# Attention outputs with the values stationary, two heads on column halves, and denominators that are spread and turned in place of the outputs

## The chip, the core and the metric

The kernel runs on one core of one Trainium2 chip. The time is the device time of one execution in microseconds, and the median of three runs before the change is 2227.28 us (2225.45 to 2228.44). Five engines run their own instruction queues and meet at semaphores: TensorE (PE; PEld is its weight load), VectorE (DVE), ScalarE (ACT), GpSimd (POOL) and SyncE (SP), which issues the loads.

## The reference, cut to what matters

A stack of four layers works on 256 tokens of width 1024, all in fp32. The first layer has a convolution and an attention to 256 memory rows (two pairs of heads) and a dense feed-forward part. The second has an attention in a window of 128 keys (12 query heads, six pairs, each head with a sink in its softmax), again two memory pairs, and a feed-forward part of eight experts. Two hybrid layers follow, each with three mixers: one of three dilated windows, one over blocks, and one to the memory, with sigmoid gates. The computation that the change touches is the same everywhere:

```python
HEAD_DIM, SEQ, BLOCK = 64, 256, 128

def memory_attention(q, q_g, mem_k, mem_v):
    q = rms_norm(q.reshape(b, s, MEM_HEADS, HEAD_DIM), q_g)
    sc = jnp.einsum('bshd,bmhd->bhsm', q, mem_k).astype(jnp.float32) * (HEAD_DIM ** -0.5)
    p = jax.nn.softmax(sc, axis=-1).astype(mem_v.dtype)
    o = jnp.einsum('bhsm,bmhd->bshd', p, mem_v)
...
# window attention: masked, biased scores, a sink beside the keys
    sink = jnp.broadcast_to(sinks..., sc.shape[:-1] + (1,))
    p = jax.nn.softmax(jnp.concatenate([sc, sink], axis=-1), axis=-1)[..., :-1]
    o = jnp.einsum('bnhgqc,bnchd->bnqhgd', p.astype(vv.dtype), vv).reshape(b, s, SWA_Q_WIDTH)
    return jnp.concatenate([o, m], axis=-1) @ w_out
...
# dilated mixer: three windows under one softmax; block mixer: causal here, since 256 tokens are one block
    w = jax.nn.softmax(jnp.stack(lses, axis=0), axis=0)
    o = jnp.einsum('gbsh,gbshd->bshd', w, jnp.stack(outs, axis=0).astype(jnp.float32))
```

## The kernel before, in words

Each engine has its program written out by hand in one block, and the order of the calls in it is the order of its queue. Tokens lie on partitions, in T = 2 tiles of P = 128; S = 256. Weights come from memory in panels of 512 KB. ScalarE rounds each to `whi` (`split_to`, L678), VectorE makes the rest `wlo` (L1195), and TensorE multiplies three products of the halves (L2083, L2136, in the hybrid layers' gates `gate`, L2646). A panel's split waits for the load, and TensorE waits for the split.

Attention goes in pairs of heads, 22 in all: two in the first layer (with other work between, `between`), eight in the window attention (six causal, two dense to the memory), six in each hybrid layer (causal, causal, the dilated pair with three causal parts, causal, dense, dense). A pair passes these steps. TensorE computes `scores` (L2222): K is 64, and the two heads of a pair lie on partitions 0 to 63 and 64 to 127, so on the two row halves of the array. VectorE masks them and takes the minimum of the negated scores (L1323). ScalarE takes the exponentials with their sums, `den`, a column for each head and token tile (`exps`, L774). TensorE turns the probabilities (`transposes`, L2241), and ScalarE and VectorE copy them to `PT` in SBUF (`copies`, L786 and L1341), so that keys lie on partitions. TensorE multiplies them with the values (`values`, L2255): a 128x128 block of probabilities is the stationary operand, 64 columns of values stream, and queries come out on partitions, six such matmuls for a causal part and eight for a dense pair. VectorE adds the sink's term to `den` (L1352, the window's heads only), takes the reciprocal of 128x4 (L1353) and multiplies the output out of PSUM with it into `att` (L1356, `scaled`). TensorE turns `att` so that head columns lie on partitions (`out_turn`, L2267, two transposes). ScalarE rounds the result to `chi` (L795) and VectorE makes `clo` (L1365), both `pair_out`. The output projections read `chi` and `clo`.

The two output banks are used in turn: `values` of a pair waits for `ofree`, which `pair_out` on VectorE counts up two pairs before. In the hybrid layers 24 gate panels are laid between the steps by hand; in the window attention nothing is laid between, and the calls are a loop over the pairs in which scores run two pairs ahead and values one behind the transposes.

Of the kernel before, what the change touches and what calls it, by code (L numbers as in the profile page):

```python
# [22 lines left out]
P = 128  # L23
T = 2
S = T * P
# [100 lines left out]
def build(nc, d):  # L126
    ctx = ExitStack()
    with ctx:
# [90 lines left out]
        tab = sb("tab", [1, 1 + MAXJOB], I32)  # L219
        assert cursor[0] <= 229344, cursor[0]  # L220
# [19 lines left out]
        class Signals:  # L240

            def __init__(self, q):
# [20 lines left out]
                self.ex = sem(q + "ex")  # L263
                self.scaled = sem(q + "scaled")
                self.oturn = sem(q + "oturn")
# [393 lines left out]
        def _(e):  # L659
# [98 lines left out]
            def attention(w, pairs, slots, out=output_bank, between=None, parts=False):  # L758
# [33 lines left out]
                def pair_out(i):  # L792

                    e.wait_ge(w.s.oturn, w.at("o", 1))
                    act(chi[:, pairs[i][3], :], out(w, w.n["o"])[:, S:2 * S], ACT.Copy).then_inc(w.s.ohi, 1)  # L795
                    w.n["o"] += 1
# [383 lines left out]
        def _(e):  # L1180
# [122 lines left out]
            def attention(w, pairs, slots, out=output_bank, scored=None, between=None, parts=False, bank=None):  # L1303
# [42 lines left out]

                def scaled(i):

                    _, _, den, sunk = pair_stats(stat, i, len(pairs[i][0]))
                    e.wait_ge(w.s.ex, w.at("a", i + 1))  # L1350
                    if pairs[i][3]:
                        w.link(v.tensor_tensor(den, den, sunk, ALU.add))  # L1352
                    w.link(v.reciprocal(den, den))  # L1353
                    e.wait_ge(w.s.pv, w.at("v", v0 - w.n["v"] + plan[i][2] // 2 + len(pairs[i][0]) + 2))
                    rows = [P, T, 2, HD]
                    v.tensor_tensor(att[:, w.n["u"] % 2, :].rearrange("p (t x k) -> p t x k", t=T, x=2),  # L1356
                                    out(w, w.n["u"])[:, 0:S].rearrange("p (t x k) -> p t x k", t=T, x=2),
                                    den.rearrange("p (x t) -> p t x", t=T).unsqueeze(3).to_broadcast(rows), ALU.mult
                                    ).then_inc(w.s.scaled, 1)
                    w.n["u"] += 1  # L1360

                def pair_out(i):
                    tile = pairs[i][4]
                    e.wait_ge(w.s.ohi, w.at("o", 1))
                    v.tensor_tensor(clo[:, tile, :], out(w, w.n["o"])[:, S:2 * S], chi[:, tile, :].bitcast(F32), ALU.subtract  # L1365
# [3 lines left out]
                if parts:  # L1369
                    return scores, copies, scaled, pair_out  # L1370
# [4 lines left out]
                for s in range(len(steps) + 2):  # L1375
# [7 lines left out]
                    if 1 <= s <= len(steps) and steps[s - 1][2]:  # L1383
                        scaled(steps[s - 1][0])
                    if s >= 2 and steps[s - 2][2]:
# [241 lines left out]
            scores, copies, scaled, pair_out = attention(  # L1627
# [9 lines left out]
            for i in range(10):  # L1637
# [10 lines left out]
                if 1 <= i < 9:  # L1648
                    scaled(i - 1)
                if i == 1:  # L1650
# [183 lines left out]
            for l in range(2):  # L1834
# [51 lines left out]
                scores, copies, scaled, pair_out = attention(  # L1886
# [1025 lines left out]
```

## Time and profile before

| | |
|---|---|
| median of three runs | 2227.28 us (2225.45 to 2228.44) |
| profiled execution: its own time, span | 2225.27 us, 2223.3 us |
| mean granted clock of TensorE | 0.997 |
| busy share of TensorE, its weight load, VectorE, ScalarE | 98%, 84%, 77%, 63% |
| memory read | 548.67 MB, 247 GB/s over the span |

The page's table of busy times and its chain are averages over stages with different limits. For each of the four places of attention the chain of waits shows what was waited for last, and the windows and forms show how full each engine was and how long one instruction took. A matmul's listed duration reaches from its start to its modelled end, so several overlap; its price is read from how far apart they start, or from a piece of the chain divided by its count. One fp32 matmul call counts as two in the trace.

### The profile page before, as it was taken

The page shows a single profiled execution, that of the slowest core. Times are in us where ns is not written, and L with a number is a line of the kernel's source. Part 1 is how long each engine was busy: PE and PEld are TensorE (multiplying, and loading weights), DVE is VectorE, ACT ScalarE, POOL GpSimd, SP SyncE. Part 2 cuts the span into 40 slices and gives each one's busy share as a digit, 9 for nine tenths or more (in the row PEclk, how much of TensorE's full clock was granted, in tenths as well). Part 3 has the DMA queues.
Part 4 walks back from the last instruction along what each step waited for, and adds up shares of the span by engine and source line. Part 5 has one row for each costly group of instructions (what it writes and reads, how often), then busy time and mean ns, then how long its engine had stood idle before and what let it go on. Part 6 is the DMA issues. An engine that isn't in the chain of part 4 may idle for free.

```text
span 2223.3 us, 36118 instructions
## 1 busy us (share of the span) xinstructions
PE 2185.2 (98%) x11690; PEld 1869.2 (84%) x11690; DVE 1716.8 (77%) x2249; ACT 1404.6 (63%) x1864; POOL 137.6 (6%) x142
## 2 busy tenths in 40 slices
PE   8999999999999999999999999999999999999998
PEld 7889987878888888888888888788889888888987
DVE  7956657699999999999999999866576556657654
ACT  4264446568787888878787878745645444564543
POOL 8400005020000000000000000000010000001000
PEclk9999999999999999999999999999999999999999
DMA  6236554279999999999999999854355655445564
GB/s 216 93 111 190 182 190 162 76 251 372 345 371 377 356 355 356 379 355 348 360 371 364 369 352 363 328 173 147 132 164 189 193 186 189 142 136 167 181 198 143
DMA packets 151054, 552.00 MB, mean 248 GB/s; under 512 B 16736, under 2 KB 16864, under 8 KB 150752
## 3 DMA queue, kind: packets, MB, share of 16 engines
q1 hardware_dynamic: 150448, 548.77, 69.6%
q8 instruction: 96, 1.57, 0.3%
q10 hardware_dynamic: 432, 1.02, 0.1%
q14 instruction: 78, 0.64, 0.1%
HBM read 548.67 MB, written 1.05 MB: 247 GB/s over the span
## 4 chain that ended last, share of the span: by engine, by line
PE 87%; issue 7%; DVE 3%; ACT 2%; POOL 0%; DMA 0%; DVEq 0%; ACTq 0%; POOLq 0%
PE L L2083 57%; PE L L2136 10%; PE L L2646 6%; PE L L2742 3%; PE TB L2151 2%; PE L L2100 2%; PE SC L2315 2%; PE L L2255 1%; DVE wlo L1195 1%; PE SC L2222 1%; PE TB L2241 1%; PE SC L2528 1%; PE SC L2536 1%; PE L L2365 1%; POOL stat L550 0%
## 5 line engine op out<-in xcount | busy, mean ns | idle before, releaser
L1195 DVE TENSOR_TENSOR wlo<-deep,whi 128x1024 fp32r<-128x1024 f32 x682 | 810.2, 1223 | 43.8 <-ACT whi L678 13.5
L678 ACT ACTIVATE whi<-deep 128x1024 fp32r<-128x1024 f32 x682 | 713.1, 1060 | 133.6 <-PE L L2083 130.0
L1195 DVE TENSOR_TENSOR wlo<-raw,whi 128x1024 fp32r<-128x1024 f32 x353 | 428.3, 1227 | 254.3 <-ACT whi L678 249.6
L678 ACT ACTIVATE whi<-raw 128x1024 fp32r<-128x1024 f32 x353 | 368.0, 1058 | 314.7 <-PE L L2083 154.6
L2083 PE MATMUL L<-whi,xhi 128*128 128x512 f32 (+1 forms) x1136 | 447.7, 394 | 3.1 <-DVE wlo L1195 2.7
L2083 PE MATMUL L<-whi,xlo 128*128 128x512 f32 (+1 forms) x1136 | 441.5, 389 | 0.0
L2083 PE MATMUL L<-wlo,xhi 128*128 128x512 f32 (+1 forms) x1136 | 441.2, 388 | 0.0
L2083 PEld LDWEIGHTS L<-whi,xhi 128*128 128x128 f32 x1136 | 213.7, 188 | 49.2 <-DVE wlo L1195 6.5
L2083 PEld LDWEIGHTS L<-whi,xlo 128*128 128x128 f32 x1136 | 213.6, 188 | 45.0
L2083 PEld LDWEIGHTS L<-wlo,xhi 128*128 128x128 f32 x1136 | 213.9, 188 | 42.0
L2083 PE MATMUL L<-whi,mhi 128*128 128x512 f32 x448 | 175.3, 391 | 0.0
L2083 PE MATMUL L<-wlo,mhi 128*128 128x512 f32 x448 | 174.6, 390 | 0.0
L2083 PE MATMUL L<-whi,mlo 128*128 128x512 f32 x448 | 174.3, 389 | 0.0
L2136 PE MATMUL L<-x2hi,whi 128*128 128x256 f32 x512 | 145.0, 283 | 0.0
L2136 PE MATMUL L<-x2hi,wlo 128*128 128x256 f32 x512 | 144.9, 283 | 0.0
L2136 PE MATMUL L<-x2lo,whi 128*128 128x256 f32 x512 | 144.9, 283 | 0.0
L2136 PE MATMUL L<-xhi,whi 128*128 128x256 f32 x448 | 128.0, 286 | 1.5 <-DVE xlo L1242 0.8
L2136 PE MATMUL L<-xhi,wlo 128*128 128x256 f32 x448 | 127.3, 284 | 0.0
L2136 PE MATMUL L<-xlo,whi 128*128 128x256 f32 x448 | 127.2, 284 | 0.0
L550 POOL TENSOR_TENSOR stat<-stat,halfneg 128x2 f32<-128x2 f32 (+3 forms) x18 | 22.4, 1246 | 1692.5 <-DVE stat L1216 1470.2
L2083 PE MATMUL L<-whi,fhi 128*128 128x512 f32 x280 | 109.7, 392 | 1.4 <-DVE wlo L1195 1.4
L2083 PE MATMUL L<-wlo,fhi 128*128 128x512 f32 x280 | 109.0, 389 | 0.0
(380 smaller groups left out, 3463.1 us busy)
## 6 DMA issues: line engine op xcount, KB each, us to landing
deep<-wm SPq DMA_DIRECT2D x679, 512.0 KB, 5.5
raw<-wm SPq DMA_DIRECT2D x245, 512.0 KB, 4.0
raw<-w SPq DMA_DIRECT2D x112, 512.0 KB, 4.3
mbuf<-mem SPq DMA_DIRECT2D x2, 1024.0 KB, 8.5
const<-const SPq DMA_DIRECT2D x1, 1312.0 KB, 8.7
out<-hn SPq DMA_DIRECT2D x2, 512.0 KB, 2.6
h<-x ACTq DMA_DIRECT2D x1, 512.0 KB, 4.9
h<-x SPq DMA_DIRECT2D x1, 512.0 KB, 4.8
```

The lines of the kernel that those rows point to most:

```text
L550: e.tensor_tensor(src, src, halfneg[:, 0:1].to_broadcast([P, n]), ALU.pow).then_inc(done, 1)
L678: act(hi, slots[:, slot, :], ACT.Copy).then_inc(w.s.hi, 1)
L1195: v.tensor_tensor(lo, slots[:, slot, :], hi.bitcast(F32), ALU.subtract).then_inc(w.s.lo, 1)
L2083: i = mm(L[2 * (g % 2) + t][:, 0:width], x[:, k, row], y[:, cols], start=(k == k0 and q == 0), stop=(k == k0 + n - 1 and q == 2))
L2100: i = mm(L[2 * (g % 2) + t][:, :], x[:, k, t * P:(t + 1) * P], y[:, kk * 512:(kk + 1) * 512], start=(k == 0 and q == 0), stop=(k == 2 * n ...
L2136: i = mm(out, x[:, cols], y[:, k, :], start=(k == 0 and q == 0 and f % 2 == 0), stop=(k == KD - 1 and q == 2 and f % 2 == 1), skip_group_c ...
L2151: i = tr(TB[w.n["t"] % 2][:, c:c + P], src, ident)
L2222: ins = mm(bank(w, x)[:, t * S:t * S + c], qkT[half, qp, t * P:(t + 1) * P], key[half, 0:c], start=True, stop=True)
L2241: ins = tr(TB[x][:, kt * S + t * P:kt * S + (t + 1) * P], tile[:, t, kt * P:(kt + 1) * P], ident)
L2315: ins = mm(SC[c % 2][:, f * S:(f + 1) * S], diag[2 * c + f][:, i, :], u[:, 2 * c + f, tap:tap + S], start=(i == 0), stop=(i == TAPS_PE - 1))
L2646: i = mm(L[2 * (bank % 2) + t][:, :], x[:, k, t * P:(t + 1) * P], y[:, kk * 512:(kk + 1) * 512], start=(k == 0 and q == 0), stop=(k == KD ...
L2742: i = mm(banks[t][:, :], x[:, k, t * P:(t + 1) * P], y[:, cols], start=(start and q == 0), stop=(stop and q == 2))
```

## The change

The operands of the values matmul change places: the values (128 keys x 64) are stationary, and the probabilities stream, 256 or 128 columns. The output is turned as it comes: head columns on partitions, the pair's first head on partitions 0 to 63 and its second on 64 to 127, so on the two column halves of the array. A causal part has four matmuls (of 256, 256, 128 and 128 columns) and a dense pair four of 256. Since queries are columns now, the denominator of a query has to stand in a column. VectorE spreads `den` over the 64 columns of each head into a new tile `dens`, 128x2x2x64 (`denominators`, with the sink's term added on the way), and TensorE turns that into the right half of the output bank ahead of the values. `scaled` then takes a reciprocal of 128x256 from PSUM into `att` and multiplies the output with it. The turn of the outputs is gone, ScalarE and VectorE read `att` in `pair_out`, and `values` waits for `scaled` two pairs before and for `den` in place of `ofree`. There is one `dens` tile; VectorE's order, `scaled` of a pair ahead of `denominators` of the next, guards it.

```diff
+        dens = sb("dens", [P, T, 2, HD], F32, region + 62464)
...
 
                 def pair_out(i):
 
-                    e.wait_ge(w.s.oturn, w.at("o", 1))
-                    act(chi[:, pairs[i][3], :], out(w, w.n["o"])[:, S:2 * S], ACT.Copy).then_inc(w.s.ohi, 1)
+                    e.wait_ge(w.s.scaled, w.at("o", 1))
+                    act(chi[:, pairs[i][3], :], att[:, w.n["o"] % 2, :], ACT.Copy).then_inc(w.s.ohi, 1)
                     w.n["o"] += 1
...
-                def scaled(i):
+                def denominators(i):
 
                     _, _, den, sunk = pair_stats(stat, i, len(pairs[i][0]))
+                    spread = lambda x: x.rearrange("p (x t) -> p t x", t=T).unsqueeze(3).to_broadcast([P, T, 2, HD])
                     e.wait_ge(w.s.ex, w.at("a", i + 1))
                     if pairs[i][3]:
-                        w.link(v.tensor_tensor(den, den, sunk, ALU.add))
-                    w.link(v.reciprocal(den, den))
+                        ins = v.tensor_tensor(dens[:, :], spread(den), spread(sunk), ALU.add)
+                    else:
+                        ins = v.tensor_copy(dens[:, :], spread(den))
+                    ins.then_inc(w.s.den, 1)
+
+                def scaled(i):
+
+                    o, to = out(w, w.n["u"]), att[:, w.n["u"] % 2, :]
                     e.wait_ge(w.s.pv, w.at("v", v0 - w.n["v"] + plan[i][2] // 2 + len(pairs[i][0]) + 2))
-                    rows = [P, T, 2, HD]
-                    v.tensor_tensor(att[:, w.n["u"] % 2, :].rearrange("p (t x k) -> p t x k", t=T, x=2),
-                                    out(w, w.n["u"])[:, 0:S].rearrange("p (t x k) -> p t x k", t=T, x=2),
-                                    den.rearrange("p (x t) -> p t x", t=T).unsqueeze(3).to_broadcast(rows), ALU.mult
-                                    ).then_inc(w.s.scaled, 1)
+                    e.wait_ge(w.s.ofree, w.at("u", 1))
+                    w.link(v.reciprocal(to, o[:, S:2 * S]))
+                    v.tensor_tensor(to, o[:, 0:S], to, ALU.mult).then_inc(w.s.scaled, 1)
                     w.n["u"] += 1
 
                 def pair_out(i):
                     tile = pairs[i][4]
                     e.wait_ge(w.s.ohi, w.at("o", 1))
-                    v.tensor_tensor(clo[:, tile, :], out(w, w.n["o"])[:, S:2 * S], chi[:, tile, :].bitcast(F32), ALU.subtract
+                    v.tensor_tensor(clo[:, tile, :], att[:, w.n["o"] % 2, :], chi[:, tile, :].bitcast(F32), ALU.subtract
                                     ).then_inc(w.s.ofree, 1)
                     w.n["o"] += 1
 
                 if parts:
-                    return scores, copies, scaled, pair_out
+                    return scores, copies, denominators, scaled, pair_out
...
                     if 1 <= s <= len(steps) and steps[s - 1][2]:
                         scaled(steps[s - 1][0])
+                    if s < len(steps) and j == 0:
+                        denominators(i)
                     if s >= 2 and steps[s - 2][2]:
                         pair_out(steps[s - 2][0])
...
                 if 1 <= i < 9:
                     scaled(i - 1)
+                if i < 8:
+                    denominators(i)
                 if i == 1:
...
                 split_to(w, p0 + 11)
                 copies(0)
+                denominators(0)
                 scores(2, 0)
                 split_to(w, p0 + 12)
                 copies(1)
                 scaled(0)
+                denominators(1)
                 scores(2, 1)
...
                 def values(i, j, later):
 
                     parts, causal = pairs[i]
+                    o = out(w, w.n["o"])
+                    if j == 0 and w.at("o", -1) > 0:
+                        e.wait_ge(w.s.scaled, w.at("o", -1))
+                    e.wait_ge(w.s.rcopy, w.at("r", 2 - 2 * later))
                     if j == 0:
-                        e.wait_ge(w.s.ofree, w.at("o", 1))
-                    e.wait_ge(w.s.rcopy, w.at("r", 2 - 2 * later))
-                    blocks = [(t, x, kt) for t in range(T) for x in range(2) for kt in range(t + 1 if causal else T)]
-                    for n, (t, x, kt) in enumerate(blocks):
-                        at = (2 * t + x) * HD
-                        ins = mm(out(w, w.n["o"])[:, at:at + HD], PT[:, w.n["v"] % 2, x, kt * S + t * P:kt * S + (t + 1) * P],
-                                 parts[j][2](x, kt), start=(j == 0 and n == 0),
-                                 stop=(j == len(parts) - 1 and n == len(blocks) - 1), skip_group_check=True)
+                        e.wait_ge(w.s.den, w.at("o", 1))
+                        for t in range(T):
+                            tr(o[:, S + t * P:S + (t + 1) * P], dens[:, t].rearrange("p x k -> p (x k)"), ident)
+                    for kt in range(T):
+                        q = kt * P if causal else 0
+                        for x in range(2):
+                            ins = mm(o[x * HD:(x + 1) * HD, q:S], parts[j][2](x, kt),
+                                     PT[:, w.n["v"] % 2, x, kt * S + q:(kt + 1) * S], start=(j == 0 and kt == 0),
+                                     stop=(j == len(parts) - 1 and kt == T - 1), skip_group_check=True)
                     ins.then_inc(w.s.pv, 1)
                     w.n["v"] += 1
                     if j == len(parts) - 1:
                         w.n["o"] += 1
 
-                def out_turn():
-
-                    e.wait_ge(w.s.scaled, w.at("u", 1))
-                    for t in range(T):
-                        ins = tr(out(w, w.n["u"])[:, S + t * P:S + (t + 1) * P], att[:, w.n["u"] % 2, t * P:(t + 1) * P], ident)
-                    ins.then_inc(w.s.oturn, 1)
-                    w.n["u"] += 1
-
                 if parts:
-                    return scores, lambda i: e.wait_ge(w.s.ex, w.at("a", i + 1)), transposes, values, out_turn
+                    return scores, lambda i: e.wait_ge(w.s.ex, w.at("a", i + 1)), transposes, values
...
                 values(1, 0, 0)
-                out_turn()
                 scores(2, 2)
                 gate(g0, 2)
-                out_turn()
                 gate(g0, 3)
```

Three places of the order. TensorE, first hybrid layer, around the second pair: the last product of a gate panel (L2646), the values (L2255), the turn of the first pair's output (L2267), the third part's scores (L2222) and the next panel. Before:

```order
L2646 MATMUL L<-whi,xlo 128x512
L2255 MATMUL L<-z,PT_81 128x64 [waits b_rcopy,b_ofree]
L2255 MATMUL L<-z,PT_81 128x64 x5
L2267 MATMUL L<-const,att 128x128 [waits b_scaled]
L2267 MATMUL L<-const,att 128x128
L2222 MATMUL SC<-qkT 128x128 [waits b_sfree]
L2222 MATMUL SC<-qkT 128x128
L2222 MATMUL SC<-qkT 128x256 x2
L2646 MATMUL L<-whi,xhi 128x512 [waits b_lo]
```

And of the changed kernel:

```order
L2655 MATMUL L<-whi,xlo 128x512
L2272 MATMUL L<-const,dens 128x128 [waits b_den,b_rcopy]
L2272 MATMUL L<-const,dens 128x128
L2276 MATMUL L<-PT_81,z 64x256 x2
L2276 MATMUL L<-PT_81,z 64x128 x2
L2238 MATMUL SC<-qkT 128x128 [waits b_sfree]
L2238 MATMUL SC<-qkT 128x128
L2238 MATMUL SC<-qkT 128x256 x2
L2655 MATMUL L<-whi,xhi 128x512 [waits b_lo]
L2655 MATMUL L<-wlo,xhi 128x512
```

Six calls of 64 columns became four of 256 and 128. The two transposes stand ahead of them, read `dens` and wait for `b_den`; the scores follow the values directly.

VectorE, window attention: copies of the fourth pair's probabilities, scaling of the third, the low part of the second pair's output, the minimum of the seventh's scores. Before:

```order
L1341 COPY PT_81<-TB 128x256 [waits a_pv,a_rdone]
L1343 COPY PT_81<-TB 128x128
L1352 TENSOR_TENSOR stat<-stat 128x4 [waits a_ex]
L1353 RECIPROCAL stat<-stat 128x4 [waits a_vd]
L1356 TENSOR_TENSOR att<-L,stat 128x256 [waits a_pv,a_vd]
L1365 TENSOR_TENSOR clo<-L,chi 128x256 [waits a_ohi]
L1323 ISA SMX,stat<-SC,zeros 128x256 [waits a_sdone,a_rdone]
L1323 ISA stat 128x1
```

And of the changed kernel:

```order
L1342 COPY PT_81<-TB 128x256 [waits a_pv,a_rdone]
L1344 COPY PT_81<-TB 128x128
L1364 RECIPROCAL att<-L 128x256 [waits a_ofree,a_pv]
L1365 TENSOR_TENSOR att<-L,att 128x256 [waits a_vd]
L1354 TENSOR_TENSOR dens<-stat 128x256 [waits a_ex]
L1371 TENSOR_TENSOR clo<-att,chi 128x256 [waits a_ohi]
L1324 ISA SMX,stat<-SC,zeros 128x256 [waits a_sdone,a_rdone]
L1324 ISA stat 128x1
```

Two instructions of 128x4 became a reciprocal of 128x256 behind the values and a spread add of 128x256 behind the multiply.

ScalarE, first hybrid layer: weight splits (L678), the evictions of the first two pairs (L795), the exponentials of the dilated pair (L774) and a gate eviction (L1058). Before:

```order
L678 ACTIVATE whi<-raw 128x1024 [waits b_used,b_raw1]
L795 ACTIVATE chi<-L 128x256 [waits b_oturn]
L678 ACTIVATE whi<-raw 128x1024 [waits b_used,b_raw2]
L795 ACTIVATE chi<-L 128x256 [waits b_oturn]
L774 ACTIVATE SMX,stat<-SMX,stat 128x3x128 [waits b_mx]
L774 ACTIVATE SMX,stat<-SMX,stat 128x3x256
L774 ACTIVATE SMX,stat<-SMX,stat 128x3x128
L774 ACTIVATE SMX,stat<-SMX,stat 128x3x256
L678 ACTIVATE whi<-raw 128x1024 [waits b_used,b_raw3]
L1058 ACTIVATE gates<-L,stat 128x512 [waits b_used]
```

And of the changed kernel:

```order
L679 ACTIVATE whi<-raw 128x1024 [waits b_used,b_raw1]
L796 ACTIVATE chi<-att 128x256 [waits b_scaled]
L679 ACTIVATE whi<-raw 128x1024 [waits b_used,b_raw2]
L796 ACTIVATE chi<-att 128x256 [waits b_scaled]
L775 ACTIVATE SMX,stat<-SMX,stat 128x3x128 [waits b_mx]
L775 ACTIVATE SMX,stat<-SMX,stat 128x3x256
L775 ACTIVATE SMX,stat<-SMX,stat 128x3x128
L775 ACTIVATE SMX,stat<-SMX,stat 128x3x256
L679 ACTIVATE whi<-raw 128x1024 [waits b_used,b_raw3]
L1059 ACTIVATE gates<-L,stat 128x512 [waits b_used]
```

Nothing moves, but the two evictions wait for VectorE's `b_scaled` where they waited for TensorE's `b_oturn`.

## Rows read from the trace of the kernel before

**Rows 1.** The page: engines busy, and the chain that ended last by line.
```profile
PE 2185.2 (98%) x11690; PEld 1869.2 (84%) x11690; DVE 1716.8 (77%) x2249; ACT 1404.6 (63%) x1864; POOL 137.6 (6%) x142
...
PE L L2083 57%; PE L L2136 10%; PE L L2646 6%; PE L L2742 3%; PE TB L2151 2%; PE L L2100 2%; PE SC L2315 2%; PE L L2255 1%; DVE wlo L1195 1%; PE SC L2222 1%; PE TB L2241 1%; PE SC L2528 1%; PE SC L2536 1%; PE L L2365 1%; POOL stat L550 0%
```

**Rows 2.** Windows: length, busy us PE, PEld, DVE, ACT, POOL, clock, DMA, GB/s.
```profile
396.00:404.00 8.00, 8.00 (x68) 6.74 (x68) 7.04 (x33) 6.98 (x28) 0.00 (x0) 1.00 0.02 4
413.00:417.00 4.00, 4.00 (x13) 3.21 (x12) 1.88 (x3) 1.33 (x2) 0.00 (x0) 0.59 0.06 7
```

**Rows 3.** Instructions by line and form: the values on TensorE (count, busy, mean ns).
```profile
L2255 PE MATMUL L<-z,PT 128*128 128x64 f32 x216 | 26.2, 271 | 0.0
...
L2255 PE MATMUL L<-mkv,PT 128*128 128x64 f32 x96 | 11.6, 274 | 1.0 <-DVE clo L1365 0.9
...
L2255 PE MATMUL SC<-mkv,PT 128*128 128x64 f32 x32 | 3.8, 271 | 0.0
```

**Rows 4.** Chain of waits, first hybrid layer: start us, us, what.
```profile
1548.76 0.23 PE L L2267 x2
...
1552.81 0.23 PE L L2267 x2
...
1553.35 2.49 ACT SMX L774 x7
...
1557.33 1.26 ACT gates L1058 x2
...
1563.61 1.06 PE SC L2222 x8
1564.68 2.95 PE L L2646 x12
...
1569.57 2.75 PE L L2646 x12
...
1583.64 1.73 PE L L2255 x16
```

**Rows 5.** Waits of TensorE, first hybrid layer: total us, times, longest.
```profile
PE L L2646 <- ACT gates L1058: 1.2, 1, 1.2
```

**Rows 6.** Chain of waits, convolution: 256-column fp32 passes.
```profile
103.09 5.62 PE SC L2315 x26
```

**Rows 7.** Instructions by line and form: VectorE (count, busy, mean ns).
```profile
L1341 DVE COPY PT<-TB 128x256 f32<-128x256 f32 x26 | 11.0, 423 | 22.6 <-PE TB L2241 22.6
...
L1343 DVE COPY PT<-TB 128x128 f32<-128x128 f32 x18 | 5.1, 281 | 0.0
...
L1353 DVE RECIPROCAL stat<-stat 128x4 f32<-128x4 f32 x22 | 3.8, 171 | 0.2
...
L1352 DVE TENSOR_TENSOR stat<-stat 128x4 f32<-128x4 f32 x6 | 0.9, 154 | 0.0
...
L1743 DVE COPY jobcur<-jobpos 128x4 f32 x4 | 0.7, 171 | 0.9 <-DVE jobcur L1804 0.5
```

**Rows 8.** Chain of waits, window attention.
```profile
385.56 0.34 DVE PT L1341
...
398.42 1.29 PE L L2255 x12
...
401.80 1.29 PE L L2255 x12
...
406.08 0.39 ACT chi L795
406.50 0.44 DVE clo L1365
406.98 2.00 PE L L2255 x16
...
412.24 0.44 DVE att L1356
412.71 0.57 PE L L2267 x2
```

More of the change, by code:

```diff
@@ L263, in __init__ @@
                 self.ex = sem(q + "ex")
+                self.den = sem(q + "den")
                 self.scaled = sem(q + "scaled")
-                self.oturn = sem(q + "oturn")
                 self.hturn = sem(q + "hturn")
@@ L1626, in _ @@
             scale(1)
-            scores, copies, scaled, pair_out = attention(
+            scores, copies, denominators, scaled, pair_out = attention(
                 w, [([sloped(SWA_PAIRS[i])], True, [nsink[:, k:k + 1] for k in SWA_PAIRS[i]], True, i) for i in range(6)]
@@ L1885, in _ @@
                 near, causal, dense = [BIG, BIG], [masked("causal")], [plain]
-                scores, copies, scaled, pair_out = attention(
+                scores, copies, denominators, scaled, pair_out = attention(
                     w, [(causal, True, near, False, 1), (causal, True, near, False, 2),
@@ L1918, in _ @@
                 copies(2)
+                denominators(2)
                 scores(3)
@@ L1927, in _ @@
                 scaled(2)
+                denominators(3)
                 scores(5)
@@ L1931, in _ @@
                 scaled(3)
+                denominators(4)
                 pair_out(2)
@@ L1935, in _ @@
                 scaled(4)
+                denominators(5)
                 pair_out(3)
@@ L2288, in attention @@
                         values(*steps[s - 1][0:2], 1 if s < len(steps) else 0)
-                    if s >= 2 and steps[s - 2][2]:
-                        out_turn()
                 w.n["a"] += len(pairs)
@@ L2419, in window_pair @@
                                                                     1024 + (2 * (p // 3) + x + 1) * HD])], True)
-            scores, scored, transposes, values, out_turn = attention(
+            scores, scored, transposes, values = attention(
                 w, [window_pair(p) for p in range(6)] + mem_pairs(8), SLOTS_SWA, parts=True,
@@ L2463, in _ @@
                     values(i - 1, 0, 1 if i < 8 else 0)
-                if i >= 2:
-                    out_turn()
             w.n["a"] += 8
@@ L2633, in _ @@
                 blocks = [([parted(6 + i, 1920 + 2 * i * HD)], True) for i in range(3)]
-                scores, scored, transposes, values, out_turn = attention(
+                scores, scored, transposes, values = attention(
                     w, [blocks[0], blocks[1], dilated, blocks[2]] + mem_pairs(12), SLOTS_HYB,
@@ L2691, in _ @@
                 values(1, 0, 0)
-                out_turn()
                 scores(2, 2)
                 gate(g0, 2)
-                out_turn()
                 gate(g0, 3)
@@ L2713, in _ @@
                 gate(g0, 3)
-                out_turn()
                 values(3, 0, 0)
@@ L2719, in _ @@
                 gate(g0, 0)
-                out_turn()
                 values(4, 0, 0)
@@ L2724, in _ @@
                 gate(g0, 1)
-                out_turn()
                 values(5, 0, 0)
                 gate(g0, 2)
-                out_turn()
                 gate(g0, 3)
```

## The prediction

> **What bounds the kernel now.** I read the page first: its table of busy times and the chain that ended last. The reader is to see one engine: TensorE busy 98% of the span, and a chain whose longest parts are weight matmuls (L2083, L2136, L2646) [rows 1]. The edited code is 22 head pairs in four places: two in the first layer (about 130 to 140 us), eight in the window attention (376 to 413 us), six in each of the two hybrid layers (about 1530 to 1594 and 1917 to 1982 us). Whoever wants to price the edit has to ask in each place who ends last.
>
> In the hybrid layers the chain runs through TensorE almost without a break: gate panels of some 2.75 to 2.95 us alternate with scores, transposes and values [rows 4]. Its one wait there is 1.2 us at a gate panel, for ScalarE's eviction of an earlier one [rows 5]; the second hybrid layer has the same row. Each nanosecond taken off TensorE there is a nanosecond of the result. The two pairs of the first layer also lie between weight matmuls on TensorE. In the window attention TensorE has no idle time while it is fed, but VectorE is at 7.04 of 8 us, so it is nearly as full [rows 2]; at that stage's end the chain hops through four engines for each pair [rows 8].
>
> **What the values cost.** An fp32 matmul of this kernel shows as two passes. There are 216 + 96 + 32 = 344 passes of 64 columns on L2255 [rows 3], 12 for a causal part (18 of them, the dilated pair having three) and 16 for a dense pair (8). On the chain 12 take 1.29 us [rows 8] and 16 take 1.73 us [rows 4], 0.108 us each. That is no cost of 64 streamed columns: passes of 256 columns go at 5.62 / 26 = 0.216 us [rows 6], so 64 would stream in 0.054; the load of 128 stationary columns sets the pace. The changed values load 64 columns and stream 256 or 128. One after the other the four matmuls of a causal part are 4 x 0.216 + 4 x 0.108 = 1.30 us and those of a dense pair 8 x 0.216 = 1.73 us: the old price, nothing won. The gain hangs on the two heads, on separate column halves, running at once. Then they are 0.65 and 0.86 us.
>
> No row shows column halves. The nearest is the scores matmul, whose two heads sit on the two row halves: 8 passes of 256 columns in 1.06 us [rows 4], where one after the other they would need 1.73 and in perfect pairs 0.86. So row halves do run at once, with 0.20 us lost on the way in. The gate panel behind them takes 2.95 us against 2.75 behind a full-array transpose [rows 4]: another 0.20 on the way out. I take both for the column halves: 1.05 us for a causal part (gain 0.24) and 1.26 us for a dense pair (gain 0.47). Bounds per part: no switching loss gives gains of 0.64 and 0.87; no pairing with switching loss gives losses of 0.41 and 0.40.
>
> The Trainium skill, "TensorEngine Tiling (Array Packing)", Key Properties, says that changing the tiling mode drains TensorE; the 0.20 us at either edge of the scores [rows 4] agrees. For column halves only the skill has a figure: "TensorE: Matmul & The Clock Gate", Part 3, gives 2.38x for three column tiles. An estimate from that page, 0.79 of ideal, would make a dense pair 1.09 instead of 0.86 us before switching and leave about half of my gain; no run here shows it yet.
>
> **Hybrid layers.** Six causal parts and two dense pairs: 6 x 0.24 + 2 x 0.47 = 2.4 us. At the second pair the values are directly followed by scores, since the turn of the outputs between them is gone; leaving column halves and entering row halves is then one switch, 0.2 us more (bounds 0 and 0.2). The two transposes a pair cost 0.23 us [rows 4] and are still two, now of denominators and ahead of the values. The wait of 1.2 us: ScalarE's eviction for the second pair stood behind the turn that TensorE did only after another gate panel (1552.81), and ScalarE's exponentials of the dilated pair queued behind it, then a weight split and the gate eviction [rows 4]. In the changed order that eviction waits for VectorE's scaling alone, which can end at about 1549.5 (the values of that pair end at 1548.76 now), and VectorE's minimum for the exponentials, which needs the next scores, at about 1551; all is some 2 us earlier, so the 1.2 us go. What is late next there is the gate panel itself. Sum 2.4 + 0.2 + 1.2 = 3.8 us a layer, 7.6 for both.
>
> What could take it back is the new wait of the values for the spread denominators, behind which all of TensorE's later work is queued. VectorE has to copy (two of 0.34), take the reciprocal, multiply and spread between the end of the transposes and the next values; a gate panel of 2.75 us lies between them, and the four come to about 0.68 + 0.42 + 0.34 + 0.34, and 0.2 for signals, 2.0. So it is hidden, with 0.7 us to spare. Without that cover, as at the window's tail, it shows in full.
>
> **First layer.** Two dense pairs: 2 x 0.47 = 0.9 us off.
>
> **Window attention.** VectorE's own bill for a causal pair: the 128x4 add (0.154) and reciprocal (0.171) [rows 7] go; a 128x256 reciprocal and a 128x256 spread come. An op of 128x256 takes 423 ns to its end [rows 7], but the next starts 0.34 us behind it, as the chain's piece for a copy shows [rows 8]; the reciprocal, whose end the multiply awaits, holds 0.42: 0.42 + 0.34 - 0.33 = +0.43 us. A period between two values is 401.80 - 398.42 = 3.38 us [rows 8], in which VectorE is busy 0.88 of the time [rows 2], 2.97 us. With 0.43 it is 3.40: about the old period, and above TensorE's, which falls to about 3.0. The stage changes its bound and the period stays near 3.4; small hand-overs of VectorE's longer queue may add 1 us over the six pairs. At the tail the old chain for each dense pair was values 2.00, turn 0.23, eviction 0.39, subtraction 0.44 [rows 4, 8], about 3.1; the new one is reciprocal 0.42, multiply 0.34, spread 0.42, signals 0.2, turn 0.22, values 1.26, together 2.9. At the very end scaling and turn (0.44 + 0.57 [rows 8]) no longer stand ahead of the output projection. So +1.0 - 0.4 - 1.0 = about -0.3 with bounds -2.5 and +1.5. The half clock (0.59 of full over four microseconds) follows this thin stretch [rows 2] and would follow it still; if it fell at another moment that is worth up to 1.7 us either way.
>
> **Sum.** -7.6 - 0.9 - 0.3 = -8.8 us on the profiled execution's 2225.27, 2216.5. The median of the runs shown is 2.0 above that execution, so 2218.5.
>
> **The reciprocal.** The sum takes 0.42 us for 128x256, one element at the pace of the copies: (423 - 281) / 128 = 1.1 ns [rows 7]. The only reciprocals in the trace are 128x4, 171 ns, and a copy of 128x4 also takes 171: no slower rate shows. But four elements are few. Read against the 128x4 add at 154 ns, the reciprocal could cost 17 / 4 = 4.3 ns an element, 1.25 us for 256. I take 0.42, since a one-source op is the nearest row, and keep 1.25 as the other end.
>
> The Trainium skill, "VectorE: DVE Perf Modes", the walkthrough of the 8-slice pipeline, speaks against the change: the reciprocal is an iterative divide on two slices with a repeat count of 8. An estimate from that page at eight times 1.1 ns an element would be 2.4 us for each of 22 reciprocals, and by it the kernel would come to about 2240. By that rule four elements should take about 30 ns more than a copy's, and the two equal rows [rows 7] do not show them.
>
> **Rivals.**
> - *The column halves run one after the other* (ends slower). For it: no row shows them, only row halves. Against it: the scores' pairs. Each part then costs 0.42 more than now: a hybrid layer 8 x 0.41 - 0.2 - 1.2 = +1.9, two +3.8; the first layer +0.8; in the window TensorE takes the bound again, 0.65 a causal and 0.87 a dense pair above my forecast, 1 us of it under VectorE's queue: -0.3 + 4.6 = +4.3. Together +8.9 on the median: 2236. It decides from the point where a dense pair takes over 1.73 us with its switches.
> - *The reciprocal is slow.* At 1.25 us, 0.83 above my value, VectorE bounds all eight window pairs: +6.6; the hybrid layers keep some of the 1.2 us wait: +1. The sum falls to -1.2, 2226: no change that can be measured. At longer ones it grows 8 us in the window for each further microsecond, and hybrid values begin to wait too, to 2236 and beyond.
> - *The gain is taken back by the denominators' wait* in the hybrid layers although the halves pair: VectorE's weight splits stand in its queue between the steps. If the values of the three last pairs wait 1 us each, 6 us return: 2224.5.
> - *The change brings no cheaper switching but better pairing:* without the 0.40 us a part, 26 parts give up to 10 us more, most of it outside the window: 2211.
>
> **How the numbers follow.** The chances are forecast 0.57, halves one after the other 0.20, slow reciprocal 0.14, denominators' wait 0.06, no switching loss 0.03. Two runs of this kernel tell about 0.2% apart, 4.5 us. The forecast's own range is 2214 to 2224; about 0.05 of its chance falls within 0.2% of before. The range over the cases is 2212 to 2237: it leaves out part of the slow reciprocal above and the cheap switching below. Faster: 0.57 - 0.05 + 0.03 = 0.55. Within: 0.05 of the forecast's edge, 0.06 of the wait and 0.04 of the reciprocal near 1.25, 0.15. Slower: 0.20 and the other 0.10 of the reciprocal, 0.30.
>
> **What would show it.** Right: pairs of 64-row-output passes that start within some ns of each other, a dense pair's values at 1.1 to 1.3 us on the chain and a causal part's near 1.05; no wait for gates in the hybrid layers; a RECIPROCAL of 128x256 near 425 ns; the window stage within 1.5 us of its old length with VectorE over 90% busy. Wrong: values at 1.7 us or above; a reciprocal of over 1 us; waits of TensorE for `dens`. The forecast as a whole is wrong if the weight matmuls behind the edited places wait for their panels, so that time won before them is lost again.

## The result and the profile after

| | before | after |
|---|---|---|
| median | 2227.16 us (2223.74 to 2228.44, 10 runs) | 2232.69 us (2229.67 to 2235.22, 10 runs) |
| profiled execution, span | 2225.27, 2223.3 | 2230.18, 2228.2 |

The ratio is 1.0031, 95% interval 1.0023 to 1.0039: slower by 5.5 us between the medians and by about 7 by the ratio, where 8.8 faster was forecast. The page of after, to be read against [rows 1]:

```profile
PE 2178.3 (98%) x11554; PEld 1844.9 (83%) x11554; DVE 1754.3 (79%) x2265; ACT 1405.8 (63%) x1864; POOL 139.4 (6%) x142
...
PE L L2099 57%; PE L L2152 10%; PE L L2655 5%; PE L L2745 3%; PE TB L2167 2%; PE L L2116 2%; PE SC L2326 2%; DVE att L1364 1%; DVE wlo L1196 1%; PE L L2276 1%; PE TB L2257 1%; PE SC L2537 1%; PE SC L2545 1%; PE L L2376 1%; PE SC L2238 1%
```

TensorE is busy for 7 us less and VectorE for 37.5 us more, and a new line of VectorE stands in the chain: `DVE att L1364`, the reciprocal of the turned denominators. The view by line and form for VectorE (count, busy us, mean ns of one), which answers to [rows 7]:

```profile
L1364 DVE RECIPROCAL att<-L 128x256 f32<-128x256 f32 x20 | 35.0, 1751 | 4.8 <-PE L L2276 4.7
...
L1365 DVE TENSOR_TENSOR att<-L,att 128x256 f32<-128x256 f32 x20 | 8.5, 425 | 0.7
...
L1356 DVE COPY dens<-stat 128x256 f32<-128x256 f32 x16 | 4.5, 283 | 0.0
...
L1364 DVE RECIPROCAL att<-SC 128x256 f32<-128x256 f32 x2 | 3.5, 1757 | 1.1 <-PE SC L2276 1.1
```

A reciprocal of 256 elements a partition takes 1.75 us; the forecast had 0.42, with 1.25 as the other end. The multiply behind it takes 0.42 us to its end, where the forecast had 0.34, and the spread copy 0.28. The chain in the first hybrid layer (start us, us, what) answers to [rows 4]:

```profile
1569.93 0.22 PE L L2272 x2
1570.15 0.80 PE L L2276 x8
1570.95 0.81 PE TB L2257 x6
1571.76 1.06 PE SC L2238 x8
1572.82 2.97 PE L L2655 x12
...
1588.61 1.68 DVE att L1364
...
1590.31 0.42 DVE att L1365
1590.74 0.21 DVE dens L1356
...
1591.08 0.41 PE L L2272 x2
1591.49 1.01 PE L L2276 x8
```

Eight passes of a causal part take 0.80 us and eight of a dense pair 1.01, where the full-array values took 1.29 and 1.73. So the column halves run in pairs, and more cheaply than forecast. But at the layer's end the reciprocal stands on the path in full, ahead of the spread for which TensorE waits. TensorE's waits over both hybrid layers (total us, times, longest), which answer to [rows 5]:

```profile
PE L L2272 <- DVE dens L1356: 2.0, 4, 0.5
PE L L2655 <- ACT gates L1059: 1.9, 2, 0.9
```

The wait for the gate eviction, which was to go, is still there (0.95 a layer), and a new one for `dens` has joined it. In the window attention VectorE is the bound. The windows (length, busy us of PE, PEld, DVE, ACT, POOL, granted clock, DMA, GB/s) and the chain at the stage's tail answer to [rows 2, 8]:

```profile
392.00:396.00 4.00, 2.70 (x12) 1.65 (x12) 3.96 (x9) 1.66 (x9) 0.12 (x1) 0.50 0.01 4
396.00:400.00 4.00, 3.48 (x18) 2.48 (x18) 2.40 (x12) 2.57 (x11) 0.00 (x0) 0.50 0.01 2
...
404.00:412.00 8.00, 4.04 (x32) 2.69 (x32) 7.93 (x22) 5.68 (x23) 0.00 (x0) 1.00 0.00 1
```

```profile
412.08 0.66 PE L L2272 x2
412.74 1.50 PE L L2276 x8
...
414.26 1.77 DVE att L1364
...
416.40 0.29 DVE dens L1356
...
416.83 0.41 PE L L2272 x2
417.24 1.04 PE L L2276 x8
...
418.30 1.77 DVE att L1364
```

VectorE is busy 7.93 of 8 us and TensorE only 4.04. The granted clock is 0.50 for two windows in a row; inside the stage, which ends at 422 us, it is at its lower level from 391.5 to 401.8 and from 412.0 to 415.4 us, 13.7 us in all. Before, it fell only behind the stage.

Where the clock is 1.00, one reciprocal follows the other in 409.48 - 404.77 = 4.71 us. The chain of after in the same stage, then that of experiment 1 below, whose copy out of PSUM stands at the reciprocal's place:

```profile
404.77 1.68 DVE att L1364
...
409.48 1.68 DVE att L1364
```

```profile
401.42 0.34 DVE att L1363
...
405.07 0.34 DVE att L1363
```

Before, two values were 3.38 us apart [rows 8]; in experiment 1 it is 3.65.

To see where the time went I took each stage's length from the trace, from the start of its first scores pass to that of its last values pass, in us. The last three columns are experiments told below.

| stage | before | after | small reciprocal | denominators early | one column half |
|---|---|---|---|---|---|
| first layer | 25.2 | 24.1 | 24.3 | 24.4 | 24.2 |
| window attention | 36.0 | 47.4 | 39.8 | 36.3 | 38.2 |
| each hybrid layer | 61.1 | 58.9 | 56.3 | 56.3 | 61.8 |
| span | 2223.3 | 2228.2 | 2212.8 | 2208.5 | 2225.4 |

The change won 1.1 us in the first layer and 2.2 in each hybrid layer, and lost 11.3 in the window attention: +5.8 in the stages and +4.9 in the span. Spans of profiled executions differ ahead of all edited code already: the first layer's scores start between 109.2 and 111.6 us in the ten traces. So small differences of whole kernels are read from the medians.

### The profile page after: what moved, and what is told of

It reads as the page before. It is cut to its first block, busy times and chain, and to the rows that moved or that the text cites. A ratio compares the mean times of both kernels' runs of the same rounds, so it can differ in the third digit from the quotient of the medians.

```text
span 2228.2 us, 35864 instructions
## 1 busy us (share of the span) xinstructions
PE 2178.3 (98%) x11554; PEld 1844.9 (83%) x11554; DVE 1754.3 (79%) x2265; ACT 1405.8 (63%) x1864; POOL 139.4 (6%) x142
## 3 DMA queue, kind: packets, MB, share of 16 engines
q10 hardware_dynamic: 432, 1.02, 0.1%
HBM read 548.67 MB, written 1.05 MB: 247 GB/s over the span
## 4 chain that ended last, share of the span: by engine, by line
PE 85%; issue 7%; DVE 5%; ACT 2%; POOL 0%; DMA 0%; DVEq 0%; ACTq 0%; POOLq 0%
PE L L2099 57%; PE L L2152 10%; PE L L2655 5%; PE L L2745 3%; PE TB L2167 2%; PE L L2116 2%; PE SC L2326 2%; DVE att L1364 1%; DVE wlo L1196 1%; PE L L2276 1%; PE TB L2257 1%; PE SC L2537 1%; PE SC L2545 1%; PE L L2376 1%; PE SC L2238 1%
```

## Experiments

**1. The reciprocal taken small.** The reciprocal goes back to the 128x4 row of denominators, ahead of the spread, and a copy stands where the large one stood, so that the multiply still has its operand in SBUF.

```diff
-                        ins = v.tensor_tensor(dens[:, :], spread(den), spread(sunk), ALU.add)
-                    else:
-                        ins = v.tensor_copy(dens[:, :], spread(den))
-                    ins.then_inc(w.s.den, 1)
+                        w.link(v.tensor_tensor(den, den, sunk, ALU.add))
+                    w.link(v.reciprocal(den, den))
+                    v.tensor_copy(dens[:, :], spread(den)).then_inc(w.s.den, 1)
...
-                    w.link(v.reciprocal(to, o[:, S:2 * S]))
+                    w.link(v.tensor_copy(to, o[:, S:2 * S]))
```

> The changed kernel with the reciprocal taken of 128x4 ahead of the spread, and a copy of 128x256 out of PSUM where the reciprocal of 128x256 stood. Everything else of the change stays: column halves, turned denominators, the same waits. Theory (the 22 reciprocals of 128x256 at 1.75 us each are the whole loss): the copy takes 0.42 us, and the time falls to what was forecast for a fast reciprocal, some 8 us below the kernel before, 2217 to 2221 us; the window stage comes back by about 10 us. Rival (the wait of the values for the spread denominators, and the longer queue, cost the time whatever the operation): it stays within 3 us of the changed kernel's 2232.7.

Measured: 2216.2 us (5 runs), before beside it 2226.04, ratio 0.9956 (0.9942 to 0.9969). It is faster than both kernels, somewhat below the 2217 to 2221 expected, and 15.4 us of span below after. Everything else of the change is still in it, so the large reciprocal, with what the clock makes of it, turned a gain of some 10 us into a loss of 7. The hybrid layers gain 4.8 us each, 1.0 more than the forecast's 3.8, and TensorE waits for nothing in them. The window attention came back by 7.6 us, where some 10 were expected, and still is 3.8 us longer than before.

The stages add up to -0.9 + 3.8 - 9.6 = -6.7 us and the span to -10.5. Of the rest, 2.3 us lie between the window's last values and the scores of the first hybrid layer (1117.7 us before, 1115.4 here), where the kernel before had its half clock, and 1.2 us lie ahead of the edited code.

**2. The reciprocal alone, on the kernel before.** One unused 128x256 reciprocal a pair ahead of the multiply.

```diff
+                    v.reciprocal(dens[:, :], out(w, w.n["u"])[:, 0:S])
                     rows = [P, T, 2, HD]
```

> The kernel before with one reciprocal of 128x256 out of PSUM added in front of each pair's multiply; its result is not used. Theory (VectorE's reciprocal alone is the loss): 1.75 us more on VectorE for each pair; in the window attention, where VectorE had about 0.4 us to spare for a pair, +10 to +13 us, in the hybrid layers 0 to 2 each: 2237 to 2243. Rival (only the changed chain through the denominators makes the reciprocal count): under 3 us more than before.

Measured: 2245.16 us, ratio 1.0087 (1.0073 to 1.0101), about 19 us, more than expected. The instruction takes 1758 ns. The window stage grew by 14.4 us, on average 1.8 for each of eight pairs, and each hybrid layer by 1.3. At full clock two values are 4.59 us apart where they were 3.38. I had left out what happens to the clock when TensorE starves: 16.3 us of the stage and 7.5 us behind it are at the lower level.

```profile
394.00:398.00 4.00, 1.51 (x12) 0.94 (x12) 3.93 (x10) 1.33 (x7) 0.00 (x0) 0.87 0.00 0
398.00:402.00 4.00, 3.88 (x19) 3.91 (x20) 2.24 (x13) 1.60 (x7) 0.00 (x0) 0.50 0.00 0
402.00:406.00 4.00, 4.00 (x19) 2.85 (x18) 3.70 (x10) 2.05 (x9) 0.00 (x0) 0.50 0.01 2
```

VectorE is full first while TensorE idles; in the next two windows the clock is at its lower level (0.50 of 2.4 GHz) and VectorE, at 2.24 of 4 us in the first, waits for TensorE.

**3. What a reciprocal costs by size.** Experiment 1 with reciprocals and copies of six sizes in SBUF added behind the last layer; one run, 2223.5 us.

```diff
+            at = 0
+            for n in (4, 16, 64, 128, 256, 512):
+                v.reciprocal(scratch[:, at:at + n], mbuf[:, 0, 0:n])
+                v.tensor_copy(scratch[:, at + n:at + 2 * n], mbuf[:, 0, 0:n])
+                at += 2 * n
```

> As small_copy, with reciprocals and copies of 4, 16, 64, 128, 256 and 512 columns in SBUF added at the very end of VectorE's program, unused, for their durations only. If the reciprocal has a rate of its own: a straight line of about 6.2 ns an element, and then 4 elements should take some 20 ns more than a copy's fixed part. If it is a fixed cost for reading PSUM: the SBUF forms are near the copies'.

VectorE's timeline (start us, us):

```profile
2214.14 0.17 DVE L2079 RECIPROCAL SMX<-mbuf 128x4 f32<-128x4 f32 x1
2214.23 0.14 DVE L2080 COPY SMX<-mbuf 128x4 f32<-128x4 f32 x1
...
2214.46 0.54 DVE L2079 RECIPROCAL SMX<-mbuf 128x64 f32<-128x64 f32 x1
...
2215.89 1.74 DVE L2079 RECIPROCAL SMX<-mbuf 128x256 f32<-128x256 f32 x1
2217.55 0.23 DVE L2080 COPY SMX<-mbuf 128x256 f32<-128x256 f32 x1
2217.69 3.34 DVE L2079 RECIPROCAL SMX<-mbuf 128x512 f32<-128x512 f32 x1
2220.95 0.37 DVE L2080 COPY SMX<-mbuf 128x512 f32<-128x512 f32 x1
```

A line: (3.34 - 0.17) / 508 = 6.24 ns an element, and 0.14 us fixed. At 4 elements the slope adds only 25 ns, little against the fixed cost. A copy of 4 elements takes 0.14 us in this form, not the 171 ns of the copy that the forecast compared with; beside its like, the small reciprocal is 0.03 us dearer.

**4. The order of the matmuls.** Experiment 1 with the loops exchanged, one head's passes first and then the other's.

```diff
-                    for kt in range(T):
-                        q = kt * P if causal else 0
-                        for x in range(2):
+                    for x in range(2):
+                        for kt in range(T):
+                            q = kt * P if causal else 0
```

> As small_copy, but the four matmuls of the values go head by head (both key tiles of the first head, then of the second) and no longer alternate between the column halves. If the halves run at once only where neighbouring calls alternate: a dense pair's values take about 1.9 us where they take 1.0 and a causal part's 1.5 where they take 0.8; 0.7 us x 12 causal parts and 0.9 x 6 dense pairs on TensorE's path outside the window, and 3 to 5 us in it, so +14 to +18 us against small_copy. Rival (TensorE's queues pair the halves whatever the order of the calls): within 2 us of small_copy. Between the two, if only the middle calls meet: about half.

Measured: 2214.84 us, ratio 0.9953 (0.9939 to 0.9967), no difference from experiment 1. A causal part takes 0.81 us and a dense pair 1.02. My expectation that pairing needs alternating calls was wrong for groups of two calls a head.

**5. Both heads on one column half.** The forecast's first rival put to the test, in the hybrid layers.

```diff
-                            ins = mm(o[x * HD:(x + 1) * HD, q:S], parts[j][2](x, kt),
+                            ins = mm(o[0:HD, q:S] if one else o[x * HD:(x + 1) * HD, q:S], parts[j][2](x, kt),
```

> The kernel with the small reciprocal, but in the two hybrid layers both heads' values go to the same column half, so that they can't run at once (outputs of these layers are not the attention's). Same number, shape and order of instructions. Theory (the gain comes from the pairing): a causal part takes 1.30 instead of 0.80 us, a dense pair 1.73 instead of 1.01, 6 x 0.50 + 2 x 0.72 = 4.4 us a layer: hybrid stages of 60.8 us and 2225 in all. Rival (most of the hybrid gain came from the turn and the wait that went): less than 2 us a layer, 2218 to 2220.

Measured: 2225.76 us, ratio 1.000 (0.9991 to 1.001): the whole gain is gone, and a hybrid layer takes 61.8 us, 5.5 more than in experiment 1 and 0.7 more than before. The chains of experiment 1 and of this one, in this order:

```profile
1579.42 1.01 PE L L2275 x8
1580.43 1.02 PE TB L2256 x8
1581.45 2.76 PE L L2654 x12
```

```profile
1584.61 1.87 PE L L2275 x8
1586.47 1.02 PE TB L2256 x8
1587.50 2.75 PE L L2654 x12
```

A dense pair goes from 1.01 to 1.87 us and a causal part from 0.80 to 1.44, each 0.14 above the expected serial price: 6 x 0.64 + 2 x 0.86 = 5.6, against 5.5 measured. The pairing is worth more than the whole gain of 4.8 us. The wait for the gates is gone in this run too, and its 1.2 us pay for a part of the edges of the column halves, 2.0 us a layer: 0.14 in each of the eight parts' values, and 0.15 on the transposes behind six of them (with a dense pair 1.02 us here and in experiment 1, 0.88 before).

**6 to 8. What still costs 3.8 us in the window attention.** All three start from experiment 1; before beside them is 2225.46 us. The first keeps the window's pairs in the old form (its diff is the old `values`, `scaled` and `out_turn` for that stage). The second spreads the denominators ahead of the copies, into two buffers:

```diff
                 if i < 8:
+                    denominators(i)
                     copies(i)
...
                     scaled(i - 1)
-                if i < 8:
-                    denominators(i)
```

The third fills TensorE's idle time with unused matmuls at two places, four calls each, and moves a wait ahead of them at either place:

```diff
+            def idle_turns(bank, n):
+
+                for _ in range(n):
+                    mm(bank[:, 0:S], ident, mkT[:, 0, :], start=True, stop=True, skip_group_check=True)
...
+                    e.wait_ge(w.s.rcopy, w.at("r", 2))
+                    idle_turns(TB[1], 4)
                     e.wait_ge(A.zrdy, 5)
-                    e.wait_ge(w.s.rcopy, w.at("r", 2))
...
+                    if i == 1:
+                        e.wait_ge(w.s.free, w.at("g", 2))
+                        idle_turns(output_bank(w, w.n["o"]), 4)
                     transposes(i, 0)
```

> The window attention's eight pairs as in the kernel before (full-array values of 64 columns, outputs scaled by rows, then turned); first layer and hybrid layers with column halves and the 128x4 reciprocal. Against the kernel with the small reciprocal everywhere (2216.2 us). Theory (in the window stage VectorE sets the pace, and column halves there only lengthen its queue): the stage returns from 39.8 to 36.0 us, but the half clock follows behind it again, so that from its start to the first hybrid layer 1.5 us are won: about 2214.5. Rival (the stage's length is given back by the clock alone): 2216. Hybrid layers 56.3 us under both.

> The kernel with the small reciprocal, but in the window attention the denominators are spread ahead of VectorE's copies of the same pair, into two buffers in turn. Theory (TensorE waits 2.7 us for the spread denominators in that stage, four times): these waits go, the stage gets 1.5 to 2.7 us shorter, 2214 to 2215. Rival (VectorE is the bound, and the order of its queue doesn't matter): 2216, the waits move to other lines.

> The kernel with the small reciprocal and, in the window attention, eight unused 128x256 matmuls of the identity (1.7 us each four) placed where TensorE waits: four ahead of the second pair's transposes, four ahead of the last head turns. Theory (the two stretches of half clock in the stage follow TensorE's idle time and cost it about 1.7 us each): the granted clock stays 1.0 there, and the stage gets 1 to 3 us shorter, 2213 to 2215. Rival (VectorE sets the pace in those stretches as well, so that a slow TensorE costs nothing): the clock stays up and the time is unchanged or 0.5 to 1 us longer by the matmuls that outlast the waits, 2216 to 2217.

| | time, us | ratio to before | window stage | stretches at half clock in it |
|---|---|---|---|---|
| before | 2225.46 | | 36.0 | none |
| window in the old form | 2216.64 | 0.9958 (0.9944 to 0.9971) | 38.5 | two |
| denominators early | 2213.9 | 0.9946 (0.9932 to 0.9960) | 36.3 | one |
| filled TensorE | 2214.57 | 0.9947 (0.9933 to 0.9960) | 37.9 | none |

A stretch is some 3.4 us at the lower level. The same code of this stage ran in experiments 1, 3 and 5, and the stage took 39.8 and 40.1 us where two stretches fell into it (1 and 3) and 38.2 where it was one (5; also 38.1 in experiment 4). So where the half clock falls moves the stage by some 2 us from one kernel to the next, and stages are compared at equal clock only. The total need not follow: the stage of experiment 4 is 1.7 us shorter than that of experiment 1, but experiment 4 has a stretch at 1440 us that experiment 1 has not, and the spans are 2212.9 and 2212.8.

The old form: 36.0 us without a stretch and 38.5 with two, against 39.8 to 40.1 for the column halves with two. The halves thus cost the stage 1.3 to 1.6 us, and the clock the rest of the 3.8. The theory's 36.0 us for the stage did not come, and the total didn't move, so the rival held for it. The window 384 to 388 us of this kernel has the values in the form of before and yet half the clock:

```profile
384.00:388.00 4.00, 4.00 (x23) 3.88 (x23) 2.16 (x12) 3.12 (x15) 0.00 (x0) 0.50 0.02 4
```

The early denominators: 36.3 us with one stretch, against 38.2, so 1.9 us won. Most of it is won at the stage's end: there the copies out of PSUM follow each other in 2.36, 2.41 and 1.45 us, and in experiment 1 in 2.89, 2.91 and 2.91. Between the causal pairs ahead of them it is 3.64 us in both. The profiled execution is the fastest of its five, 2210.48 us. TensorE's waits from 370 us to the stage's end, experiment 1 first, then the early denominators:

```profile
PE TB L2256 <- DVE PT L1344: 3.0, 2, 2.0
PE L L2271 <- DVE dens L1356: 2.7, 4, 1.5
...
```

```profile
PE TB L2257 <- DVE PT L1346: 4.8, 3, 2.6
...
```

The wait for `dens` is gone, and 1.8 us came back as a wait for VectorE's copies, since VectorE remains nearly full (3.70 to 3.92 of 4 us in each window from 388 to 408).

The filled TensorE: the window 384 to 388 us, experiment 1 first, then the filled one.

```profile
384.00:388.00 4.00, 4.00 (x24) 2.70 (x23) 3.18 (x15) 3.32 (x17) 0.00 (x0) 0.57 0.00 0
```

```profile
384.00:388.00 4.00, 4.00 (x31) 2.73 (x29) 3.93 (x22) 3.87 (x18) 0.00 (x0) 1.00 0.02 4
```

With the clock at 1.00 VectorE is busy 3.93 instead of 3.18 us: at half clock it had waited for TensorE. The stage is 1.9 us shorter than with two stretches but only 0.3 shorter than with one, where the theory gave 1 to 3. Its span of 2214.5 is 1.7 us longer than that of experiment 1: the half clock is gone from the stage, but the trace has it for 6.8 us at 70 us, where experiment 1 has 3.4, and for 3.4 at 1442. The intervals of the three ratios and of experiment 1's overlap, so the totals don't rank these four. The early denominators have the lowest median; their interval lies below 1, as do those of the other three.

## Why the prediction was wrong

The step that failed is the one under "The reciprocal": 0.42 us for 128x256 "since a one-source op is the nearest row". It is 1.75 us, outside both ends that I had set from rows. The two equal rows, 171 ns for a 128x4 reciprocal and for a 128x4 copy [rows 7], were read as "no slower rate shows". They are no like pair: in experiment 3 a reciprocal and a copy of 4 elements with the same source take 0.17 and 0.14 us, and the slope's part of the first is 25 ns. The other end divided the reciprocal's 17 ns over the add by four, and that difference of two nearly equal numbers was no bound.

The Trainium skill, "VectorE: DVE Perf Modes", the walkthrough of the 8-slice pipeline, has the reciprocal as an iterative divide with a repeat count of 8, and the estimate of 2.4 us from that page gave about 2240. Experiment 3 agrees in kind, a cost for each element far above a copy's, and in size lies at 6.24 ns an element, 5.7 times the 1.1 ns that the estimate multiplied by eight. At four elements the page's rule asked for about 30 ns over a copy, and the like pair of experiment 3 has 0.03 us, though copies of 4 and 16 elements differ by as much (0.14 and 0.11). The forecast used two rows that are not alike to set the rule aside.

With 1.75 us put in, the forecast's own bill gives the period of the window attention: 2.97 + 0.43 + (1.75 - 0.42) = 4.73 us, and 4.71 was measured at full clock. That step was right but for its one term. The length of the stage fits less well than it seems. 8 x 1.33 = 10.6 on top of -0.3 is +10.3, and +11.3 was measured, but that is partly luck: from experiment 1, which had +3.8 with two stretches at half clock, the same 10.6 would lead to +14.4, and the reciprocals added 7.6 with twice as much half clock in the stage. How the rest divides stays open.

In the hybrid layers the budget of 2.0 us under a gate panel of 2.75 becomes 3.3. TensorE's waits for `dens` are four of some 0.5 us, at the two dense pairs of each layer; a layer lost 2.6 us against experiment 1, of which the waits for `dens` and gates show 2.0.

- *Values.* Right in direction, too dear: 0.80 and 1.01 us measured for 1.05 and 1.26. The loss on entry is 1.01 - 0.86 = 0.15 us, not the 0.20 of row halves [rows 4], and the one on the way out, for which I added 0.20 to every part, is paid by what stands behind: 0.15 on six transposes (0.81 us for 0.66). With both edges a causal part costs 0.95 us and a dense pair 1.16.
- *Hybrid layers.* Mechanism right, and with a cheap reciprocal 4.8 us each instead of 3.8. The values give 6 x 0.48 + 2 x 0.72 = 4.3, six edges behind them take back 0.9, and the wait adds 1.2, which makes 4.6. The wait for the gate eviction goes, as forecast, and returns only when the reciprocal delays what ScalarE waits for.
- *First layer.* -0.9 forecast, -1.1 measured.
- *Window attention.* The forecast's -0.3 (its terms add up to -0.4) includes 1.0 us won behind the last values, which the stage's length leaves out. Up to the next scores experiment 1 has 3.8 - 2.3 = +1.5. Its period of 3.65 us is again VectorE's bill: 2.97 + 0.34 for the copy + 0.30 for the spread = 3.61, since it keeps the small add and reciprocal that the forecast struck out. That is what the halves cost among the causal pairs; at the stage's end it is TensorE's wait for the spread denominators, which the early denominators remove. The rest is the half clock, which fell inside the stage twice, where the prediction had it only behind. The prediction's reading that TensorE has no idle time while it is fed came from 396 to 404 us; earlier in the stage it idled before the change too, with VectorE nearly full:

```profile
384.00:388.00 4.00, 2.01 (x21) 1.79 (x17) 3.88 (x21) 3.66 (x17) 0.00 (x0) 1.00 0.13 51
```

- *Sum.* -8.8 forecast; with the small reciprocal 0.44% (0.31 to 0.58) was measured, about -9.8. That the two are near is partly luck: the hybrid layers brought 2.0 us more than forecast and the window attention 1.8 less.
- *Rivals.* The slow reciprocal, at 0.14, was the true one, at a size beyond its 1.25 us. By its rule, 8 us for each further microsecond, 1.75 us gives -1.2 + 4.0 = +2.8, about 2230, and the hybrid waits come on top; 2232.69 was measured. Halves one after the other, at 0.20, was refuted by the chain of after (0.80 and 1.01 us), and experiment 5 shows what it would have cost. The wait for `dens` occurred, 1.0 us a layer, but as a consequence of the reciprocal. The one without switching loss did not hold: the edges cost 0.15 us each instead of 0.20.

## What to carry to other kernels

A row with very few elements tells an instruction's fixed cost and next to nothing of its rate; before a small operation is made wide, ask for its price by element, and where no row has it, keep a wide upper end. Keep the expensive operation on the compact data and spread its result: here this turned 7 us of loss into 10 of gain. Small matmuls of two heads on column halves paid in the stages where TensorE was the bound. Where VectorE was, TensorE's gain became idle time; in such a stage compare at equal clock, and look where else in the trace the half clock went.

## What the runs showed that was not expected

- VectorE's fp32 reciprocal costs 6.24 ns an element a partition and 0.14 us fixed (0.17 us at 4 elements, 3.34 at 512), the same from PSUM (1751 ns) as from SBUF (1.74 us) at 256. The SBUF copy of 256 took 0.23 us.
- Passes on two column halves run at once in both orders of the calls that were tried (0.80 and 0.81 us for a causal part). On one half the same passes take 1.44.
- Where the half clock falls differs between kernels that have the same code in the stage: 38.2 us with one stretch in it, 39.8 and 40.1 with two. Unused matmuls in the gaps kept the granted clock at 1.00 there, though TensorE was busy for only 2.05 of 4 us from 408 to 412. What decides its place in two otherwise equal kernels stays open.
